# State-space outputs from rows by channel and lag, full-size chunk-sum weights, and the skip inside the lag-0 kernel

## The reference

```
def _s5_core(ug, lb_re, lb_im, bb_re, bb_im, c_re, c_im):     # ug: (T, G, 16), G = 128 groups
    bu = einsum('tgc,gpc->tgp', ug, bb)                         # 16 channels -> 64 complex states
    x_t = lb * x_(t-1) + bu_t                                   # associative scan over t
    return einsum('tgp,gcp->tgc', xr, c_re) - einsum('tgp,gcp->tgc', xi, c_im)

u = h @ w_in                                                    # 2048 x 2048
y = _s5_core(u) + d_skip * u
g = gelu(y);  g = g * sigmoid(g @ w_gate);  out = g @ w_out
```

## Time and profile before

| | |
|---|---|
| median of 3 runs | 2722.25 us (2720.71 to 2724.89) |
| the profiled execution | 2721.67 us, span 2719.9 us |
| PE busy | 2649.9 us, 97% of the span |
| DVE, ACT, POOL busy | 2280.5, 1293.8, 516.3 us |
| a round in the middle of `ssm_in` | 9.63 us |

### The profile page before, as it was taken

How to read it: one execution, slowest core, us unless ns; L and a number is a source line. 1 busy time by engine, 2 the same in 40 slices (tenths; PEclk the granted TensorE clock), 3 DMA queues, 4 the chain that set the end, 5 groups by cost and what they waited for, 6 DMA issues and landing times.

```text
span 2719.9 us, 50038 instructions
## 1 busy us (share of the span) xinstructions
PE 2649.9 (97%) x18416; PEld 2375.2 (87%) x18416; DVE 2280.5 (84%) x3379; ACT 1293.8 (48%) x1869; POOL 516.3 (19%) x468
## 2 busy tenths in 40 slices
PE   5999999999999999999999999999999999999998
PEld 1998888888898888888888999999888888888887
DVE  6978988888889998899998988998898975677754
ACT  2444444444434655435555344444365553455543
POOL 4142201101133111000111321244411110011122
PEclk8999999999999999999999999999999999999999
DMA  9979989888866887678887968878777755655663
GB/s 378 395 258 342 345 311 344 312 316 327 318 231 219 322 286 249 207 249 305 281 281 265 376 229 251 241 256 322 255 246 250 265 180 188 201 188 189 185 191 117
DMA packets 242267, 725.47 MB, mean 267 GB/s; under 512 B 51106, under 2 KB 60066, under 8 KB 241186
## 3 DMA queue, kind: packets, MB, share of 16 engines
q1 hardware_dynamic: 185184, 666.46, 70.7%
q10 hardware_dynamic: 56900, 56.54, 6.5%
HBM read 701.66 MB, written 25.44 MB: 267 GB/s over the span
## 4 chain that ended last, share of the span: by engine, by line
PE 82%; DVE 5%; issue 1%; POOL 1%; DMA 1%; ACT 1%; ACTq 0%; DVEq 0%; SPq 0%; POOLq 0%
PE proj L1929 21%; PE proj L1956 19%; PE proj L1936 11%; PE proj L1959 10%; PE proj L1979 5%; PE proj L1981 4%; PE proj L1980 4%; PE proj L1974 2%; PE proj L1961 1%; DVE w_lo L1202 1%; PE proj L1977 1%; ACT w_hi L606 1%; DVE work L1485 1%; PE ps L2102 1%; PE ps L2192 1%
## 5 line engine op out<-in xcount | busy, mean ns | idle before, releaser
L606 ACT ACTIVATE w_hi<-raw 128x1024 fp32r<-128x1024 f32 (+1 forms) x896 | 929.9, 1043 | 1110.8 <-PE proj L1936 327.7
L1202 DVE TENSOR_TENSOR w_lo<-raw,w_hi 128x1024 fp32r<-128x1024 f32 (+1 forms) x896 | 1105.0, 1238 | 348.5 <-ACT w_hi L606 337.0
L1956 PE MATMUL proj<-h_hl,w_hi 128*128 128x512 f32 x2025 | 514.0, 394 | 2.7 <-DVE x L1532 1.8
L1929 PE MATMUL proj<-h_hl,w_hi 128*128 128x512 f32 x2096 | 499.9, 391 | 0.0
L1929 PEld LDWEIGHTS proj<-h_hl,w_hi 128*128 128x128 f32 x2096 | 385.7, 188 | 74.8
L1956 PEld LDWEIGHTS proj<-h_hl,w_hi 128*128 128x128 f32 x2025 | 369.9, 189 | 71.9 <-DVE x L1532 2.1
L1092 DVE SCALAR_TENSOR_TENSOR ada<-ada,held 128x1024 f32<-128x1024 f32 x304 | 391.9, 1289 | 0.0
L1835 POOL TENSOR_TENSOR a_hl<-work,a_hl 128x256 fp32r<-128x256 f32 (+1 forms) x88 | 122.4, 1391 | 1134.2 <-ACT a_hl L896 1134.2
L1959 PEld LDWEIGHTS proj<-h_hl,w_lo 128*128 128x128 f32 x2160 | 295.5, 191 | 21.3
L1959 PE MATMUL proj<-h_hl,w_lo 128*128 128x256 f32 x2160 | 301.9, 283 | 0.0
L1936 PEld LDWEIGHTS proj<-h_hl,w_lo 128*128 128x128 f32 x2096 | 268.7, 191 | 10.2
(11 more groups left out here) (287 smaller groups left out, 3391.6 us busy)
## 6 DMA issues: line engine op xcount, KB each, us to landing
raw<-in_w_up SPq DMA_DIRECT2D x352, 512.0 KB, 4.9
ada<-in_ada_t SPq DMA_DIRECT2D x304, 512.0 KB, 5.6
raw<-in_w_in SPq DMA_DIRECT2D x224, 512.0 KB, 6.4
raw<-in_w_down SPq DMA_DIRECT2D x128, 448.0 KB, 4.2
raw<-in_w_down SPq DMA_DIRECT2D x64, 512.0 KB, 3.7
ada<-in_ada_w SPq DMA_DIRECT2D x48, 512.0 KB, 9.3
raw<-in_w_out SPq DMA_DIRECT2D x32, 512.0 KB, 5.3
raw<-in_ssm_w_in SPq DMA_DIRECT2D x32, 512.0 KB, 4.9
```

Source lines behind the costliest of these rows:

```text
L606: nc.scalar.activation(w_hi[:, j % LAG, 0:nk * P], raw[:, j % s.ring, 0:nk * P], ACT.Copy).then_inc(hi_ready, 1)
L1202: V.tensor_tensor(w_lo[:, j % LAG, 0:nk * P], raw[:, j % s.ring, 0:nk * P], w_hi[:, j % LAG, 0:nk * P].bitcast(F32), ALU.subtract).then_in ...
L1929: mm(proj[b % 2][:, :], w_hi[:, j % LAG, (k - k0) * P:(k - k0 + 1) * P], hl[:, k].rearrange("p c t -> p (c t)"), start=(k == 0), stop=False)
L1956: ins = mm(both, w_hi[:, j % LAG, w], hl[:, k].rearrange("p c t -> p (c t)"), start=(k == 0), stop=False)
```

## The change

The lag kernels are no longer spread by DVE into 128x128 block-diagonal weights. ACT copies four shifted windows of them out of PSUM (`spread_lags`), writes them to HBM (`kw_d`) and SP reads them back (`load_taps`) as weights `lagged` with rows (channel, position), the rows that `u_rows` has; the output products of that part are 16 of 32 weight columns and 64 data columns. The skip is added to the lag-0 kernel by one more small product with the identity, so `skip` is gone and `gelu` reads PSUM. `bp` is loaded into tiles of 128x128 that hold the two groups side by side with zeros between, so `chunk_sums` has half as many products, of twice the size each way. `magnitudes` goes from POOL to ACT. The loads of `bp`, `cp` and `tab` go from ACT's queue to SP's (but for blocks 0 and 1), and `kernels_of` runs a round sooner (step 2n+3).

```
 def chunk_sums(n):
-    pe.wait_ge(bp_ld[n % 2], 16 * (n // 2 + 1))
+    pe.wait_ge(bp_ld[n % 2], 32 * (n // 2 + 1))
     for q in range(4):
         for r in range(2):
-            for g in range(2):
-                rows = slice(g * SP_, (g + 1) * SP_)
-                ins = mm(e_ps[n % 2][rows, r, q, :], bp[rows, n % 2, q, r, :], u_rows[rows, n % 2, q, :],
-                         start=True, stop=True)
+            ins = mm(e_ps[n % 2][:, r, q, :], bp[n % 2][:, q, r].rearrange("p g s -> p (g s)"), u_rows[:, n % 4, q, :],
+                     start=True, stop=True)
 def kernels_of(n):
-    wait(pe, kd_made, n - 1)
+    pe.wait_ge(s5_clear, 3)
+    pe.wait_ge(kw_made, n + 1)
     for q in range(4):
+        rows = slice(32 * q, 32 * q + 32)
         for r in range(2):
-            ins = mm(k_ps[n % 2][32 * q:32 * q + 32].rearrange("p (k o) -> p k o", k=CHUNK),
-                     bst[:, n % 2, q, r, :], cp[:, n % 2, q, 0:CHUNK, r * SC:(r + 1) * SC],
-                     start=(r == 0), stop=(r == 1))
+            mm(k_ps[n % 2][rows, :, 0:CHUNK], bst[:, n % 2, q, r, :],
+               cp[:, n % 2, q, 1:1 + CHUNK, r * SC:(r + 1) * SC].rearrange("p k o -> p o k"),
+               start=(r == 0), stop=False)
+        ins = mm(k_ps[n % 2][rows, :, CHUNK - 1], ident[:, rows], d_own[:, n, :], start=False, stop=True)
 def outputs(n):
-    pe.wait_ge(kd_made, n + 1)
+    pe.wait_ge(lag_ld[n % 2], 32 * (n // 2 + 1))
-    wait(pe, ypre_done, n - 1)
+    wait(pe, gelu_done, n - 1)
-    for k in range(CHUNK):
-        mm(y[:, k * NCH:T], kd[:, n % 2, k].rearrange("p g o -> p (g o)"),
-           u[:, n % 4, 0:CHUNK - k, :].rearrange("p j a -> p (j a)"), start=(k == 0), stop=False)
+    for j in range(CHUNK):
+        for q in range(4):
+            mm(y[32 * q:32 * q + 32, j * NCH:(j + 1) * NCH], lagged[:, n % 2, q].rearrange("p g (o k) -> p (g o) k", k=CHUNK)[:, :, CHUNK - 1 - j],
+               u_rows[:, n % 4, q, :], start=(j == 0), stop=False)
-    late.setdefault(2 * n + (4 if n == KT - 1 else 5), []).append(kernels_of(n))
+    late.setdefault(2 * n + 3, []).append(kernels_of(n))
...
+def spread_lags(n):                                   # ACT, step 2n+8
+    act.wait_ge(kb_done, n + 1)
+    wait(act, kw_out[n % 2], 16 * (n // 2))
+    nc.scalar.activation(lag_rows[:, n % 2], k_windows[n % 2], ACT.Copy).then_inc(kw_made, 1)
+    wait(act, lag_ld[n % 2], 32 * (n // 2))
+    act.wait_ge(kw_made, n + 3)
+    act.dma_start(kw_d[n % 2].rearrange("(p j) f -> p (j f)", j=CHUNK),
+                  lag_rows[:, n % 2].rearrange("p j o k -> p (j o k)")).then_inc(kw_out[n % 2], 16)
+def load_taps(n):                                     # SP, step 2n+12
+    wait(sp, y_done, n - 1)
+    sp.wait_ge(kw_out[n % 2], 16 * (n // 2 + 1))
+    by_group = kw_d[n % 2].rearrange("(q g m) f -> g m q f", q=4, g=2)
+    for g in range(2):
+        sp.dma_start(lagged[g * SP_:(g + 1) * SP_, n % 2, :, g, :], by_group[g]).then_inc(lag_ld[n % 2], 16)
+def load_bp(n):                                       # SP, step 2n+9
+    wait(sp, e_done, n - 1)
+    for g in range(2):
+        rows = slice(g * SP_, (g + 1) * SP_)
+        sp.dma_start(bp[n % 2][rows, :, :, g].rearrange("p q r s -> p (q r) s"),
+                     bp_d[n][rows].rearrange("p (m s) -> p m s", s=SP_)).then_inc(bp_ld[n % 2], 16)
```

239 lines of the change are left out of this document (130 added, 109 removed).

## The result

The change made the kernel slower: 2739.27 us (median of 6 runs, 2735.6 to 2747.57) against 2721.39 us (6 runs beside them, 2718.78 to 2724.89), a ratio of 1.0070 with the 95% interval 1.0059 to 1.0080. The forecast was 2721.6, no change, and its range ended at 2736. The profiled execution of after took 2735.6 us, the shortest of its six, with a span of 2733.8 against 2719.9; so the two profiles show 13.9 us of the 17.9 between the medians, and the rest has to come from runs. Part of that gap is scatter of the stages ahead: the stage begins at 1615.26 us of the span after and at 1618.34 before (over all the profiles of this case from 1613.9 to 1620.1). From there to the first product behind `gate` are 269.9 us after and 253.1 before, +16.8.

What follows compares the result with a forecast made beforehand. PE's own work was taken to bound the stage; rounds gave -0.2 us, and +0.5 - 0.4 + 0.3 - 0.3 - 0.6 at start and end made -0.7, so 2721.6 us as median, no change; range 2709 to 2736.

Steps and rivals of the forecast that it cites:

- Chunk sums: PE's chunk-sum group: 16 records of 128x128 weights at 0.111 us each, 1.90 us instead of 1.29, +0.61 a round.
- the rival of hidden loads: Chunk sums: 128x128 weight loads hidden, records every 0.058 us, 13.6 us faster in all, 2708 us; chance 0.15.
- The part with u: Output products from u_rows: eight sets of four abreast plus the array's split, 0.67 us instead of 1.36, -0.69 a round.
- the bound of 0.111 a set: Part with u: if stepped weights made each of 8 sets cost 0.111 us instead of 0.057, +0.43 a round.
- The new identity products: Kernels group: 8 records of 16 columns for the skip, taken as two sets, +0.07 us a round.
- the lag kernels themselves ... keep their number and size: Kernels group: the existing lag-kernel products were given no added time; the c_wide part likewise.
- What reads with a step: Stepped weights, data operand and result: 0 taken; bound +0.43 and +0.22 us a round, +10.4 in all.
- What has to be in time: Lag weights and u_rows land before PE wants them, narrowly: 0 taken, 0.7 us a round as upper bound.
- Start and end: Stage's first and last blocks: +0.5, -0.4, +0.3, -0.3, and -0.6 for the last xst wait.
- The sum: All terms together: -0.7 us against the profiled 2721.67; with the median 0.6 higher, 2721.6 us, no change.
- Transfers late: Rival: lag weights or u_rows land after PE wants them, 0.5 us a round, +7.5, 2729 us; chance 0.20.
- steps not free: Rival: stepped operands slow PE's products by half to all of 10.4 us, 2727 to 2732 us; chance 0.18.

Runs made afterwards that it cites:

- e5: The changed kernel with the chunk sums put back as pairs of 64x64 products on the same wide tiles; ratio 1.0065 to the kernel before.
- e7: The changed kernel with paired 64x64 chunk sums, bp in 2 KB runs, lag kernels lag by lag, contiguous data, column groups in turn, identity last; ratio 1.0048.
- e4: The changed kernel with the lag-kernel products issued column groups in turn, identity products last; kernels group 0.70 us, ratio 1.0072.
- e1: The changed kernel with the lag-kernel products' data operand read 16 numbers side by side, result still stepped; kernels group 0.79 us, ratio 1.0071.
- e2: The changed kernel with lag kernels laid out lag by lag in PSUM, so data operand and result are both contiguous; kernels group 0.79 us, ratio 1.0067.
- e16: e7 with lag-kernel products, their cp load, window copy and widening of C each one step (half a round) earlier; ratio 1.0023.
- e13: The changed kernel with neither write nor read of the lag windows from block 2 on (output not the reference's); 2729.66 us, ratio 1.0037.
- e12: e7 with neither write nor read of the lag windows from block 2 on (output not the reference's); ratio 0.9993.
- e9: e7 with the read of the lag windows issued by ScalarE instead of SP, one step after their write; ratio 1.0029.
- e14: e9 with the loads of bp, cp with bst, and tab issued by ScalarE, leaving SP weight pieces alone; ratio 1.0040.
- e15: e9 with the read of u_rows issued first in ScalarE's step, ahead of gelu, window copy and widening of C; ratio 1.0045.
- e6: e2 with bp landing as one 2 KB run a partition, 128 packets in place of 1,024 (output not the reference's); ratio 1.0062.

## Why the prediction was wrong

By its own steps:

- *Chunk sums*, +0.61: measured +0.58 (1.87 against 1.29). Right (+0.54 in most rounds), from weight loads of 0.11 us; the rival of hidden loads (2708) is out. e5 gives the same from the other side, 1.70 to 1.08.
- *The part with u*, -0.69: measured -0.61. Right in kind; a set with stepped weights takes 0.065 to 0.07 us instead of 0.056. What the bound of 0.111 a set would have cost isn't seen.
- *The new identity products*, "two sets: +0.07", and "the lag kernels themselves ... keep their number and size": **the step that failed.** The group grew by 0.87 to 0.88 us a round. I counted the 24 records in sets of four abreast without looking at the order in which the code issues them: one column group after another, with the identity product as the last of each. The same records with the groups in turn and contiguous data cost +0.00 (e7). As written, the order costs 0.55 us (e4) and the step 0.46 (e1). The rows gave no warning: the kernel before has the same order with two products in each column group, and 0.38 us for its 16 records.
- *What reads with a step*, 0 taken, +0.22 as the bound for the kernels: mis-sized even at the bound. I applied the price of a weight load (0.111) to a data operand. The data operand's step costs 0.46 in the order of after and 0.33 with the groups in turn (0.70 against 0.37); the weights' step next to nothing, the result's step nothing. The Trainium skill ("Advanced Engine Details and Errata", Memory Cachelines) says that reads that never hit a line twice are slower, and the runs agree for the data operand; it says also that any gap in a PSUM pattern slows matmuls, and e1 against e2, both 0.79 us, don't.
- *What has to be in time*: (the addends up to the window copy give T + 2.6 and not 2.7, which changes nothing) the margins of 1.0 us for the lag weights and 1.3 for `u_rows` were worked out with landings of the kernel before (4.7 and 5.1). For the lag weights the margin held: their write took 5.5 us and their read 2.9 instead of 5.1, and PE never waits for `kw_d` after. For `u_rows` the landing rose to 6.1, and PE waits for them twice, 0.6 us. SP standing at the write for up to 7.1 us was seen as something that delays only what is behind it, with 3 us or more to spare. Weight pieces had that to spare in every profile; `bp` had not, at the stage's end (2.3 us), nor had `bst` once the rounds were shorter. Where the standing goes (e7 to e16), weight pieces land in 5.6 us instead of 6.6 and `u_rows` in 4.7 instead of 6.6. The refill of instructions, 4.1 us of waits in e7, was in no term. Beside PE's round of 10.41 the loss is small in the profile (3.4 us) and about 9 us between medians (after against e13).
- *Start and end*: -0.6 was taken for the wait of 1.23 us for the last `xst`. That wait is gone, but one of 2.29 us for the last `bp` has come, with a granted clock of 0.50 behind it.
- *The sum*: PE's excess 0.78 a round in place of -0.01 makes 11.7 us, 9.4 between medians (e13), and the trip the rest. "Transfers late" (priced at 7.5 us) and "steps not free" (up to 10.4) had 0.20 and 0.18, each priced alone; both came in part, together with an order that no rival named, and the range excluded both together.

That the PE terms are worth their 9.4 us only as long as nothing else binds is also shown: e1 to e5 took 7 to 10 us of PE's work out and moved the time by nothing that the intervals show; a shorter round leaves less time for the same landings, and the waits grew from 3.4 to between 8.4 and 15.2 us. The two bounds lay close together: 10.41 us of PE's work a round, and about 10.1 as the round of e7 with waits. What is open: how the waits of after are spread over runs other than the profiled one, and what delays the instruction refills, which are nearly half of the 11 us that e12 keeps with both suspects gone (`u_rows` are 3.9 of them).

## What to carry to other kernels

Before products with 32-column weights are counted as four abreast, read the order in which they are issued and how the data operand is read: with three products in each column group, one group after another and data with a step, the group took 1.25 us; with the groups in turn, the closing product included, and data side by side, 0.37. A queue that waits for a landing is charged with everything behind it: issue the cause of the wait half a round sooner (e16) rather than move the wait to another engine that other work needs (e9 gained less, and e14 and e15 nothing more). When the profile books a wait under "issue", look for what landed just before it ended: here it was either a load whose semaphore the view didn't name, or the refill of the engine's own instructions. And when a stage shows no waits, ask how much shorter it may become before a chain of write and read binds: here a round of 9.63 had such a chain just hidden, and one of 9.02 had not.

## What the runs showed that I had not expected

- A stepped PSUM result (7 numbers apart) costs nothing against 64 side by side: 0.79 us both.
- A weight operand with a step of four numbers costs 0.01 us a set of four records, while a data operand with a step of 32 nearly doubles a group (0.70 against 0.37 us).
- 256 KB more in each of 13 rounds, copied from DRAM to DRAM in runs of 1 KB and 256 bytes, left the kernel before at 1.0001; 896 packets of 256 bytes fewer in each round of e6 changed nothing either.
- PE stopped in the middle of a weight piece, with nothing to wait for but its own instructions (3.35 us in e7), and the granted clock was 0.50 for 3.15 us behind it. At the end of the stage after, the wait of 2.29 us did the same; the windows show PEclk 0.50 from 1793 to 1795 us:

```profile
1793.00:1795.00 2.00, 2.00 (x11) 2.00 (x11) 1.10 (x2) 0.00 (x0) 0.00 (x0) 0.50 0.30 64
```
